# Conditioning blocks in runs of four, and the state store issued from SyncE

## The chip, the core and the metric

The kernel runs on one NeuronCore of a Trainium2 chip. The metric is the device time of one execution in microseconds (us); the time before is the median of three executions. A profiled execution gives the rows shown further down; times inside it count from the start of its span.

## The reference, cut to what matters

One inference step of a two-layer trunk over 128 context and 256 latent tokens, width 1024. Layer 0 mixes tokens with a bidirectional state-space scan (SSD: 32 heads of width 64, 8 groups, state 128, chunks of 128 tokens), layer 1 with a gated delta rule; each is followed by a convolutional feed-forward. All sub-layers are modulated by vectors that come from a condition:

```python
def adaln_params(cond, w_ada, b_ada):
    ada = (jax.nn.silu(cond) @ w_ada + b_ada)[:, None, :]
    return tuple(jnp.split(ada, 6, axis=-1))
...
# ssd_scan, one direction
decay = jnp.exp(jnp.where(mask, seg, -jnp.inf))
y_intra = jnp.einsum('bcijgr,bcjgrp->bcigrp', scores[..., None] * decay, xdt)
states = jnp.einsum('bcqgn,bcqgr,bcqgrp->bcgrpn', bc, decay_end, xdt)
y_inter = jnp.einsum('bcign,bcgrpn,bcigr->bcigrp', cc, s_prev, jnp.exp(acum))
```

The final states of the context scan are outputs of their own (`new_state_ssd_fwd`, `new_state_ssd_bwd`). The product with `w_ada` (2 layers x 6 x 1024 columns, 96 blocks of 1024x128 in float32, 512 KB each) uses only two condition vectors, so it is nearly all weight traffic.

## The kernel before, in words

The first 16 blocks of `w_ada` are used ahead of layer 0. The other 80 are used inside the SSD scan, `ADA_G`: ten in each of its eight groups g = 0 to 7. Every engine has its program written out by hand; they meet only at semaphores.

**Buffers and loads.** Weight blocks go through `raw`, `RAW` = 4 buffers used in turn. `load_block` (L252, its DMA is L259) runs on SyncE (SP) and waits until the block four places earlier has been used (`ada_used`), so block 4 of a group is asked for when its block 0 is used, and block 0 of the next group when block 6 is. `ssd_sp` (L884) issues, per group: the load of the next group's start states `s0` (L895, 256 KB), then ten block loads.

**TensorE (`ssd_pe`, L1054).** A group covers three token chunks, u = 3g, 3g+1, 3g+2. `turn_rows` (L1065, L1066) transposes a chunk into PSUM bank 0 and waits for `s_gm` of the chunk before; `segment` (L1075, L1076) makes the decay exponents; `states` (L1086) the group's context states; `entry_decays` (L1099) the decays at chunk entry, and with k = 0 it waits until ScalarE has copied the states out (`s_stout`), since it overwrites their bank; `entry` (L1111) the part of the output that comes from the entry state; `outputs` (L1124) the part inside the chunk. `conditioning(g, lo, hi)` (L1130) runs blocks lo to hi of the group's ten through `ada_block` (L369, 8 matmuls a block, each block after the wait for its load). `ada_columns` (L376) ends the group after ScalarE has copied the ten rows out (L396).

Between `segment(u+1)` and the group's end the order before is: states, blocks 0-1, entry_decays 0, outputs u, blocks 2-3, turn_rows u+3, segment u+2, entry_decays 1, blocks 4-5, entry 0, turn_rows u+4, blocks 6-7, outputs u+1, turn_rows u+5, segment u+3, entry 1, blocks 8-9, outputs u+2, ada_columns. In the last group the runs are 0-1, 2-4, 5-7, 8-9, with no `turn_rows`, no `segment(u+3)` and no run after entry 1.

**ScalarE (`ssd_act`, L900).** In order: `decays` (exp of a segment, L913), `state_out` (L919, states to `st_sb`), `rows_lo` (L946, eight activations, `seg_lo`), the store of `st_sb` to `o_ssd` (L962, its own DMA queue), `entry_decays` (L925), `token_rows` (L909, `xtok`), `decays`, `gates_out` (L931 or L935, L937), `entry_decays`, `rows_lo`, `token_rows` twice, `decays`, `rows_lo`, `ada_rows` (L396). `state_out` of the next group waits until the store has landed (`s_out`).

**VectorE (`ssd_dve`).** `masked` (L1177, `gm_s`) follows `xtok` of its chunk and frees PSUM bank 0 for the next `turn_rows`; `entered` (L1203, L1204, L1206) takes the result of `entry`. VectorE runs `entered(g, 0)` ahead of `masked(u+4)`.

After the last group SyncE has loaded the first blocks of `w_out`; ScalarE rounds them to the high part (`whi`, L277), GpSimd makes the low part (`wlo`, L287), and the output product (L327) starts.

Of the kernel before, what the change touches and what calls it, by code (L numbers as in the profile page):

```python
# [49 lines left out]
SSD_H, SSD_P, SSD_G = 32, 64, 8  # L50
# [68 lines left out]
def trunk(nc, io):  # L119
    ctx = ExitStack()  # L120
    with ctx:
        def sem(name):
            return ctx.enter_context(nc.semaphore(name))
# [62 lines left out]
        def v(name):  # L186
            a, b = VEC[name]
            return vec[:, a:b]
# [63 lines left out]
        def load_block(sp, p, j):  # L252
            b = j + p.raw0
            if j.i is not None or j.base >= RAW:
                sp.wait_ge(ada_used if p.kind == "ada" else lo_ready, (j + (p.own0 - RAW + 1)).val)
            elif b.base >= RAW:
                s, count = used(b.base - RAW)
                sp.wait_ge(s, count + 1)
            sp.dma_start(raw[:, b.mod(RAW), 0:p.kt * P], p.src[j.val]).then_inc(raw_in[b.mod(RAW)], 16)  # L259
# [5 lines left out]
        def load_first(sp, p):  # L265
            for k in range(RAW):
                load_block(sp, p, Idx(k))
# [11 lines left out]
        def split_first(act, name):  # L279

            for k in range(2):
                split_hi(act, phase[name], Idx(k))
# [112 lines left out]
        def ada_rows(act, bank, n):  # L395
            act.activation(arow[:, :], ps[:, bank, 0:P], ACT.Copy).then_inc(ada_row, 1)  # L396
# [438 lines left out]
        def tmp(name, shape, dt=F32):  # L835
            t = put(name, shape, dt, at=st[0])
            st[0] += nbytes([P] + list(shape[1:]), dt)
            assert st[0] <= rows_at, (name, st[0], rows_at)
            return t
# [13 lines left out]
        st_sb = tmp("st_sb", [P, 512])  # L853
        ADA_G = tuple(10 * g for g in range(SSD_G)) + (ADA_2,)
        s_s0 = [sem(f"s_s0{k}") for k in range(2)]
        s_out = [sem(f"s_out{k}") for k in range(2)]
# [20 lines left out]
        def ssd_begin(eng):  # L877
            eng.wait_ge(dt_last, 1)
            eng.wait_ge(tok_split, 2)
            eng.wait_ge(dt_dec, 1)  # L880
            eng.wait_ge(conv_silu, 2 + CONV_T)
            eng.wait_ge(blk_done, phase["ssd_in"].own0 + N_IN + SPL)

        def ssd_sp(sp):  # L884
            p = phase["ada_rest"]
            load_first(sp, p)
            ssd_begin(sp)
            sp.dma_start(s0[:, 0, :, :], io["s_ssd"][0]).then_inc(s_s0[0], 16)
            for g in range(SSD_G):
                b = g % 2  # L890
                if g + 1 < SSD_G:
                    if g:
                        sp.wait_ge(s_in, 2 * g)
                        sp.wait_ge(s_dec, 2 * g)
                    sp.dma_start(s0[:, 1 - b, :, :], io["s_ssd"][g + 1]).then_inc(s_s0[1 - b], 16)  # L895
                for j in range(ADA_G[g] + RAW, min(ADA_G[g + 1] + RAW, ADA_2)):
                    load_block(sp, p, Idx(j))
            load_first(sp, phase["ssd_out"])

        def ssd_act(act):  # L900
            ssd_begin(act)

            def token_rows(u):
                g, c = u // 3, u % 3
                act.wait_ge(s_a, u + 1)
                if g >= 2:
                    act.wait_ge(s_xdt, u - 5)
                    act.wait_ge(s_st, 2 * g - 2)
                act.activation(xtok[:, g % 2, c, :], ps[:, 0, 0:TOK], ACT.Copy).then_inc(s_xtok, 1)  # L909

            def decays(u):
                act.wait_ge(s_seg, u + 1)
                act.activation(ps[:, 1 + u % 2, :], ps[:, 1 + u % 2, :], ACT.Exp).then_inc(s_exp, 1)  # L913

            def state_out(g):
                act.wait_ge(s_st, 2 * g + 1)
                if g:
                    act.wait_ge(s_out[(g - 1) % 2], 16 * ((g - 1) // 2 + 1))
                act.activation(st_sb[:, :], ps[:, 4, :], ACT.Copy).then_inc(s_stout, 1)  # L919

            def entry_decays(g, k):
                act.wait_ge(s_eb, 2 * g + k + 1)
                if g:
                    act.wait_ge(s_bw, 2 * g - 1 + k)
                act.activation(e_in[:, k].rearrange("p d n -> p (d n)"), ps[:, 4 + k, :], ACT.Exp).then_inc(s_ee, 1)  # L925

            def gates_out(g):
                act.wait_ge(s_v, 3 * g + 3)
                for t in (2 * g, 2 * g + 1):
                    if g == 0:  # L930
                        act.activation(rms_sum[t % 2][:, :], gate[:, t, :], ACT.Square).then_inc(rms_sq, 1)  # L931
                    else:
                        if g > 1:
                            act.wait_ge(rms_add, t - 3)
                        act.activation(rms_new[t % 2][:, :], gate[:, t, :], ACT.Square).then_inc(rms_sq, 1)  # L935
                for t in (2 * g, 2 * g + 1):
                    act.activation(yhi[:, t, :], gate[:, t, :], ACT.Copy, scale=nw[:, t:t + 1]).then_inc(y_hi, 1)  # L937

            def rows_lo(u):
                g, c = u // 3, u % 3  # L940
                if u:
                    act.wait_ge(s_seg, u)
                for d in range(2):
                    for h in range(4):
                        n = 4 * g + 32 * d + h
                        i = act.activation(seg_lo[:, d, h * P:(h + 1) * P], masks[:, 1 + d, :], ACT.Copy,  # L946
                                           scale=tok_lo[:, c, n:n + 1].bitcast(F32))
                i.then_inc(s_rlo, 1)

            nw = v("ssd_norm")  # L950
            rows_lo(0)
            for c in range(NCH):
                token_rows(c)
            decays(0)
            rows_lo(1)
            for g in range(SSD_G):
                more = g + 1 < SSD_G
                decays(3 * g + 1)
                state_out(g)
                rows_lo(3 * g + 2)  # L960
                act.wait_ge(s_stout, g + 1)
                act.dma_start(io["o_ssd"][g], st_sb[:, :].rearrange("p (d n) -> p d n", d=2)).then_inc(s_out[g % 2], 16)  # L962
                entry_decays(g, 0)
                if more:
                    token_rows(3 * g + 3)
                decays(3 * g + 2)
                if g:
                    gates_out(g - 1)
                entry_decays(g, 1)
                if more:  # L970
                    rows_lo(3 * g + 3)
                    token_rows(3 * g + 4)
                    token_rows(3 * g + 5)
                    decays(3 * g + 3)
                    rows_lo(3 * g + 4)
                act.wait_ge(ada_used, ADA_1 + ADA_G[g + 1])
                act.wait_ge(ada_tr, g + 1)
                ada_rows(act, 3, ADA_G[g + 1] - ADA_G[g])
            split_first(act, "ssd_out")
            gates_out(SSD_G - 1)  # L980
# [73 lines left out]
        def ssd_pe(pe):  # L1054
            ssd_begin(pe)
            p = phase["ada_rest"]
# [73 lines left out]
            def conditioning(g, lo, hi):  # L1130
                if lo == 0:
                    pe.wait_ge(ada_ready, g + 2)
                count = ADA_G[g + 1] - ADA_G[g]
                for n in range(min(lo, count), min(hi, count)):
                    ada_block(pe, Idx(p.raw0 + ADA_G[g] + n), 3, n, count)
# [4 lines left out]
            for g in range(SSD_G):  # L1140
                u = 3 * g
                segment(u + 1)
                last = g + 1 == SSD_G
                states(g)
                conditioning(g, 0, 2)
                entry_decays(g, 0)
                outputs(u)
                conditioning(g, 2, 5 if last else 4)
                turn_rows(u + 3)
                segment(u + 2)  # L1150
                entry_decays(g, 1)
                conditioning(g, 5 if last else 4, 8 if last else 6)
                entry(g, 0)
                turn_rows(u + 4)
                conditioning(g, 8 if last else 6, 10 if last else 8)
                outputs(u + 1)
                turn_rows(u + 5)
                if g + 1 < SSD_G:
                    segment(u + 3)
                entry(g, 1)  # L1160
                if g + 1 < SSD_G:
                    conditioning(g, 8, 10)
                outputs(u + 2)
                pe.wait_ge(ada_row, g + 2)
                ada_columns(pe, ADA_G[g + 1] - ADA_G[g], 3)
# [1529 lines left out]
```

## Time and profile before

| | |
|---|---|
| median of three executions | 1739.4 us (1738.55 to 1741.45) |
| the profiled execution's own time | 1738.55 us |
| its span, first to last instruction | 1736.8 us |
| TensorE busy | 1590.8 us, 92% of the span |
| mean granted TensorE clock | 0.952 of full speed |
| SSD scan on TensorE | about 255 to 426 us |

A group is known by its number g. Its start is the first `states` matmul: 288.89, 308.65, 328.42, 348.17, 367.91 and 387.66 us for g = 1 to 6. "Landing" is the time from the issue of a DMA to its last byte's semaphore.

### The profile page before, as it was taken

What the parts mean: (1) busy time and instruction counts of PE and PEld (TensorE: products, weight loads), DVE (VectorE), ACT (ScalarE), POOL (GpSimd) and SP (SyncE); (2) the same over time, 40 slices, a digit from 0 to 9 for tenths busy, and PEclk for the clock granted to TensorE, in tenths of its full rate; (3) what the DMA queues carried; (4) which work ended last, traced back from release to release, by engine and by line L of the source; (5) the groups of instructions that cost most, each with busy time, mean ns of one, the idle gap of its engine ahead of it and who ended that gap; (6) DMA issues with size and microseconds to landing.
All of it is one profiled execution on the core that took longest, in us unless ns stands there. A gap on an engine that the chain in (4) does not pass through costs nothing.

```text
span 1736.8 us, 31461 instructions
## 1 busy us (share of the span) xinstructions
PE 1590.8 (92%) x11787; PEld 1484.4 (85%) x11787; DVE 909.6 (52%) x1753; ACT 765.7 (44%) x1370; POOL 911.0 (52%) x516
## 2 busy tenths in 40 slices
PE   4999999998978999998799999988988969999995
PEld 2999987777968999997699999878788949999994
DVE  1533105666237777523733455778873266777424
ACT  2555436765224444323546553544443334444322
POOL 1455555775533555553345555777563515555551
PEclk6999999999998999999899999899879979999998
DMA  8333336888322333432223232000013313343420
GB/s 326 105 111 127 128 122 221 290 297 274 110 85 79 127 123 131 143 124 73 97 98 110 98 100 66 18 14 25 14 50 109 121 48 109 121 132 131 134 100 36
DMA packets 54969, 205.26 MB, mean 118 GB/s; under 512 B 6096, under 2 KB 6096, under 8 KB 54352
## 3 DMA queue, kind: packets, MB, share of 16 engines
q1 hardware_dynamic: 53712, 201.70, 34.7%
q10 hardware_dynamic: 1152, 2.10, 0.3%
q8 instruction: 73, 1.20, 0.3%
q14 instruction: 32, 0.26, 0.0%
HBM read 196.44 MB, written 7.34 MB: 117 GB/s over the span
## 4 chain that ended last, share of the span: by engine, by line
PE 50%; issue 23%; POOL 12%; DVE 7%; ACT 6%; DMA 1%; POOLq 0%; DVEq 0%; SPq 0%; ACTq 0%
POOL wlo L287 12%; PE ps L327 5%; PE ps L329 5%; PE ps L328 5%; PE ps L780 4%; PE ps L782 4%; PE ps L781 4%; PE ps L2379 3%; PE ps L2381 3%; PE ps L2380 3%; ACT seg_lo L946 2%; PE ps L369 1%; PE ps L1471 1%; PE ps L1086 1%; PE ps L1573 1%
## 5 line engine op out<-in xcount | busy, mean ns | idle before, releaser
L287 POOL TENSOR_TENSOR wlo<-raw,whi 128x1024 fp32r<-128x1024 f32 (+1 forms) x201 | 511.2, 2544 | 496.7 <-ACT whi L277 496.7
L277 ACT ACTIVATE whi<-raw 128x1024 fp32r<-128x1024 f32 (+1 forms) x250 | 275.2, 1102 | 603.9 <-PE ps L329 376.7
L327 PE MATMUL ps<-hhi,whi 128*128 128x384 f32 x704 | 238.5, 339 | 25.5 <-DVE hlo L434 25.4
L328 PE MATMUL ps<-hlo,whi 128*128 128x384 f32 x704 | 236.5, 336 | 0.0
L329 PE MATMUL ps<-hhi,wlo 128*128 128x384 f32 x704 | 236.5, 336 | 0.0
L611 DVE SCALAR_TENSOR_TENSOR evac<-ps,vec,evac 128x189 f32<-128x189 f32 (+3 forms) x440 | 166.4, 412 | 101.7 <-ACT evac L562 72.0
L2168 POOL TENSOR_TENSOR wlo<-raw,whi 128x1024 fp32r<-128x1024 f32 x49 | 118.2, 2413 | 140.5 <-ACT whi L277 140.5
L544 DVE SCALAR_TENSOR_TENSOR xr<-xr,evac 128x384 f32 x32 | 64.1, 2004 | 195.1 <-ACT evac L513 193.9
L327 PEld LDWEIGHTS ps<-hhi,whi 128*128 128x128 f32 x704 | 133.0, 189 | 31.2 <-issue 29.8
L2379 PE MATMUL ps<-hhi,whi 128*128 128x384 f32 x392 | 140.4, 358 | 12.9 <-DVE hlo L434 12.3
L780 PE MATMUL ps<-hhi,whi 128*128 128x384 f32 x392 | 133.3, 340 | 10.2 <-DVE hlo L434 9.6
L328 PEld LDWEIGHTS ps<-hlo,whi 128*128 128x128 f32 x704 | 133.4, 189 | 0.0
L329 PEld LDWEIGHTS ps<-hhi,wlo 128*128 128x128 f32 x704 | 133.2, 189 | 0.0
L2381 PE MATMUL ps<-hhi,wlo 128*128 128x384 f32 x392 | 132.7, 339 | 0.0
L2380 PE MATMUL ps<-hlo,whi 128*128 128x384 f32 x392 | 132.7, 338 | 0.0
L782 PE MATMUL ps<-hhi,wlo 128*128 128x384 f32 x392 | 132.1, 337 | 0.0
L781 PE MATMUL ps<-hlo,whi 128*128 128x384 f32 x392 | 132.1, 337 | 0.0
L327 PE MATMUL ps<-ghi,whi 128*128 128x384 f32 x352 | 121.3, 345 | 1.3 <-POOL wlo L287 1.3
L329 PE MATMUL ps<-ghi,wlo 128*128 128x384 f32 x352 | 117.6, 334 | 0.0
L328 PE MATMUL ps<-glo,whi 128*128 128x384 f32 x352 | 117.6, 334 | 0.0
L327 PE MATMUL ps<-yhi,whi 128*128 128x384 f32 x256 | 90.3, 353 | 3.5 <-POOL wlo L287 3.5
L2379 PEld LDWEIGHTS ps<-hhi,whi 128*128 128x128 f32 x392 | 74.6, 190 | 19.1 <-issue 16.4
(306 smaller groups left out, 3426.2 us busy)
## 6 DMA issues: line engine op xcount, KB each, us to landing
raw<-w_in_in SPq DMA_DIRECT2D x98, 512.0 KB, 3.5
raw<-w_ada_in SPq DMA_DIRECT2D x96, 512.0 KB, 4.9
raw<-w_up_in SPq DMA_DIRECT2D x88, 512.0 KB, 3.4
raw<-w_down_in SPq DMA_DIRECT2D x32, 704.0 KB, 4.1
raw<-w_out_in SPq DMA_DIRECT2D x32, 512.0 KB, 3.4
s<-s_ssd_in SPq DMA_DIRECT2D x8, 256.0 KB, 4.9
o_ssd_out<-st_sb ACTq DMA_DIRECT2D x8, 256.0 KB, 2.3
S<-s_gdn_in SPq DMA_DIRECT2D x4, 512.0 KB, 3.4
```

Of the source, the lines that this page charges most:

```text
L277: act.activation(whi[:, s.mod(SPL), 0:p.kt * P], raw[:, b.mod(RAW), 0:p.kt * P], ACT.Copy).then_inc(hi_ready, 1)
L287: pool.tensor_tensor(wlo[:, s.mod(SPL), 0:p.kt * P], raw[:, b.mod(RAW), 0:p.kt * P], whi[:, s.mod(SPL), 0:p.kt * P].bitcast(F32), ALU.subt ...
L327: pe.matmul(out, a, rhi[:, h, :], start=(r == 0), stop=False)
L328: pe.matmul(out, a, rlo[:, lo_tile(r) if lo_tile else r, :], start=False, stop=False)
L329: mm = pe.matmul(out, b, rhi[:, h, :], start=False, stop=(r == q * p.kt - 1))
L611: i = dve.scalar_tensor_tensor(x, y, w, x, ALU.mult, ALU.add)
L780: pe.matmul(out, a, hhi[:, k, :], start=(k == 0), stop=False)
L781: pe.matmul(out, a, hlo[:, k, :], start=False, stop=False)
L782: mm = pe.matmul(out, b, hhi[:, k, :], start=False, stop=(k == DT - 1))
L2379: pe.matmul(out, a, hhi[:, k, :], start=(k == 0), stop=False)
L2380: pe.matmul(out, a, hlo[:, k, :], start=False, stop=False)
L2381: mm = pe.matmul(out, b, hhi[:, k, :], start=False, stop=(k == DT - 1))
```

## The change

SyncE takes the store over from ScalarE: for each group it waits for `s_stout` after the load of `s0` and issues the store ahead of the group's ten block loads. On TensorE the ten blocks run as 0-3 behind `states`, 4-7 behind entry_decays 1, and 8-9 behind entry 1; in the last group as 0-3 and 4-9. Matmuls, loads and bytes are the same in number and kind.

```diff
@@ ssd_sp
                     sp.dma_start(s0[:, 1 - b, :, :], io["s_ssd"][g + 1]).then_inc(s_s0[1 - b], 16)
+                sp.wait_ge(s_stout, g + 1)
+                sp.dma_start(io["o_ssd"][g], st_sb[:, :].rearrange("p (d n) -> p d n", d=2)).then_inc(s_out[b], 16)
                 for j in range(ADA_G[g] + RAW, min(ADA_G[g + 1] + RAW, ADA_2)):
@@ ssd_act
                 rows_lo(3 * g + 2)
-                act.wait_ge(s_stout, g + 1)
-                act.dma_start(io["o_ssd"][g], st_sb[:, :].rearrange("p (d n) -> p d n", d=2)).then_inc(s_out[g % 2], 16)
                 entry_decays(g, 0)
@@ ssd_pe
                 segment(u + 1)
-                last = g + 1 == SSD_G
                 states(g)
-                conditioning(g, 0, 2)
+                conditioning(g, 0, 4)
                 entry_decays(g, 0)
                 outputs(u)
-                conditioning(g, 2, 5 if last else 4)
                 turn_rows(u + 3)
                 segment(u + 2)
                 entry_decays(g, 1)
-                conditioning(g, 5 if last else 4, 8 if last else 6)
+                conditioning(g, 4, 8 if g + 1 < SSD_G else 10)
                 entry(g, 0)
                 turn_rows(u + 4)
-                conditioning(g, 8 if last else 6, 10 if last else 8)
                 outputs(u + 1)
```

## Rows read from the trace of the kernel before

**Rows 1.** The page: span, busy time, granted TensorE clock in 40 slices of 43.4 us.

```profile
span 1736.8 us, 31461 instructions
...
PEclk6999999999998999999899999899879979999998
```

**Rows 2.** Busy time by window: PE, PEld, DVE, ACT, POOL, then clock, DMA share, GB/s.

```profile
288.90:308.65 19.75, 19.02 (x295) 15.68 (x294) 13.52 (x29) 13.79 (x38) 12.48 (x13) 1.00 0.85 297
...
407.40:430.00 22.60, 17.31 (x277) 13.44 (x276) 13.22 (x29) 11.09 (x24) 9.63 (x7) 1.00 0.77 269
```

**Rows 3.** TensorE's timeline in group 1: start, length, line, operation, [idle before].

```profile
288.89 1.89 PE L1086 MATMUL ps<-xw,xtok 128*128 128x256 f32 x8
290.71 1.08 PE L369 MATMUL ps<-raw,scond 128*32 128x128 f32 x32
...
297.28 1.08 PE L369 MATMUL ps<-raw,scond 128*32 128x128 f32 x32
298.29 1.16 PE L1111 MATMUL ps<-proj,s 128*128 128x128 f32 x8
...
299.93 1.08 PE L369 MATMUL ps<-raw,scond 128*32 128x128 f32 x32
300.94 1.09 PE L1124 MATMUL ps<-ge_s,xdt 128*64 128x128 f32 x16
302.51 0.55 PE L1065 MATMUL ps<-masks,proj 128*128 128x128 f32 x3 [0.47 <-DVE gm_s L1177]
```

**Rows 4.** ScalarE's timeline in group 1, around the store, and its later L946.

```profile
289.95 0.60 ACT L919 ACTIVATE st_sb<-ps 128x512 f32<-128x512 f32 x1 [0.28 <-PE ps L1086]
...
290.58 0.34 ACTq L962 DMA_DIRECT2D o_ssd_out<-st_sb  x1
290.74 2.14 ACT L946 ACTIVATE seg_lo<-masks,tok_lo 128x128 fp32r<-128x128 f32 x7
...
295.43 0.49 ACT L909 ACTIVATE xtok<-ps 128x384 f32<-128x384 f32 x1 [1.98 <-PE ps L1066]
...
299.18 2.44 ACT L946 ACTIVATE seg_lo<-masks,tok_lo 128x128 fp32r<-128x128 f32 x8
```

**Rows 5.** VectorE's timeline in group 1: `masked(u+3)`, start of `entered(g, 0)`, `masked(u+4)`.

```profile
295.96 0.42 DVE L1177 TENSOR_TENSOR gm_s<-ps,masks 128x256 f32<-128x256 f32 x1 [1.16 <-ACT xtok L909]
...
300.10 0.42 DVE L1203 TENSOR_TENSOR ps<-ps,e_in 128x256 f32<-128x256 f32 x1
...
302.03 0.42 DVE L1177 TENSOR_TENSOR gm_s<-ps,masks 128x256 f32<-128x256 f32 x1 [0.72 <-ACT xtok L909]
```

**Rows 6.** Loads of blocks 4 and 5 of group 1, then of its blocks 6 and 7.

```profile
L259 SPq DMA_DIRECT2D raw<-w_ada_in x2: 327/362/396, 291.4 to 291.9; - x2
DMA to landing us min/median/max: 3.7/4.7/5.6
L259 SPq DMA_DIRECT2D raw<-w_ada_in x2: 327/619/911, 294.3 to 294.8; - x2
DMA to landing us min/median/max: 4.4/4.8/5.2
```

**Rows 7.** Loads of blocks 6 and 7 of group 6.

```profile
L259 SPq DMA_DIRECT2D raw<-w_ada_in x2: 328/348/368, 393.1 to 393.5; - x2
DMA to landing us min/median/max: 4.9/5.3/5.7
```

**Rows 8.** Loads of group 3's blocks 2 and 3, issued at the end of group 2.

```profile
L259 SPq DMA_DIRECT2D raw<-w_ada_in x2: 328/348/367, 325.5 to 325.9; - x2
DMA to landing us min/median/max: 4.2/5.0/5.8
```

**Rows 9.** DMA traffic in 40 slices of 288.89 to 308.65 us.

```profile
GB/s 423 415 402 390 158 340 203 133 274 315 307 423 390 373 323 415 373 365 323 141 191 182 282 307 373 357 274 224 323 265 390 431 423 207 108 66 116 232 257 406
```

**Rows 10.** The end of the last group: PE's timeline, then the chain that ended last.

```profile
428.96 0.44 PE L327 MATMUL ps<-yhi,whi 128*128 128x384 f32 x1 [2.60 <-POOL wlo L287]
...
419.17 6.23 DMA raw<-w_out_in
```

## The prediction

> **What bounds the kernel now.** I read the page first: the span is 1736.8 us in 40 slices of 43.4 us, and TensorE is granted nearly its full clock after the first slice [rows 1]. The diff touches only the SSD scan, so next came the busy time by window, one window for each group; that of group 1 stands for six. What to see there: a group takes 19.75 us, TensorE is busy for 19.0 of it at a granted clock of 1.00, which is the 2.4 GHz level, and the DMA engines are 85% busy at 297 GB/s; only the last group is longer [rows 2]. So the scan is TensorE's, with DMA close behind. Any gain must come out of the 0.7 us in a group in which TensorE is idle, and a loss can come from loads.
>
> TensorE's timeline shows where that idle time is: 0.47 us before `turn_rows(u+5)`, for `gm_s` [rows 3]. `gm_s` itself waits for ScalarE's `xtok`, which stands behind the eight L946 activations of 2.44 us [rows 4, 5]. That chain starts where `segment(u+2)` ends, and the change leaves the same TensorE work ahead of that point (four blocks, entry_decays 0, outputs u, turn_rows). I take from this that the period of 19.75 us stays as it is unless a load comes late.
>
> **The store.** The part that goes: one wait and one DMA issue on ScalarE per group. The issue is 0.34 us long, but it runs beside the activations: seven L946 beside it take 2.14 us, 0.306 each, and eight without a store beside them 2.44 us, 0.305 each [rows 4]. The gain on ScalarE is 0. The wait costs nothing either, since `st_sb` is ready at 290.55 when the issue comes at 290.58.
>
> What is added on SyncE: a wait for `s_stout`, behind which the group's ten block loads queue, and for them TensorE waits. It ends at 290.55; the first load behind it can't go before block 0 is used and went at 291.4 [rows 4, 6]. The issue ends near 290.6 + 0.34 = 290.95, still 0.45 us ahead, so the wait costs 0. Uncovered, it would delay the load of block 4, which landed at 291.4 + 3.7 = 295.1 and is needed at 297.28, 2.2 us later [rows 3, 6].
>
> The Trainium skill (DMA: Bandwidth & Descriptors, section "Issuing engines are not separate DMA queues") says that issuing from several engines saves only the sequencer's issue time, as all queues run on the same 16 DMA engines. By that rule alone, taking the store off ScalarE's queue would be worth up to 8 x 0.34 = 2.7 us; the rows above put it at 0, because the issue lies beside activations that are as long without it.
>
> **Blocks 0-3.** Blocks 2 and 3 now run right behind 0 and 1, ahead of entry_decays 0 and outputs u. A run of two takes 1.01 us (299.93 to 300.94), so 0.507 a block [rows 3]: counted from the group's start, block 2 is needed at 1.82 + 1.01 = 2.83 and block 3 at 3.34. Their loads are asked for when blocks 8 and 9 of the group before are used, which doesn't move. The worst pair was issued at 325.5 and 325.9 and landed at 329.7 and 331.7 [rows 8]; group 3 starts at 328.42, so it needs them at 331.25 and 331.76: 0.06 us to spare. This is the tightest of seven such pairs; in the other six block 3 landed 0.5 to 1.5 us ahead of its new need. Cost 0. Entry_decays 0 and outputs u come 1.01 us later. VectorE, which idles 1.16 us behind them, before `masked(u+3)`, and ScalarE, idle 1.98 us between its `e_in` and the next `xtok`, absorb that [rows 4, 5]; the tighter has 0.15 us left.
>
> **Blocks 4-7.** This is where I expect the cost. All four must now be in by the time TensorE has reached them: 4 at 297.28, that is 8.39 from the start, then 8.90, 9.40 and 9.91. Before, blocks 6 and 7 were wanted from 299.93, 11.04 from the start [rows 3]. Their loads can be asked for 1.9 us earlier (block 2 was used by about 294.1 and its buffer's next load was issued at 294.3, against 292.4 now, as block 2 is used by 288.89 + 3.34 [rows 3, 6]), but an earlier request helps only if the DMA engines are free.
>
> They were not. A 512 KB block at the peak rate of about 415 GB/s takes 1.27 us [rows 9]. In group 1 blocks 4 to 7 landed at 295.1, 297.5, 298.7 and 300.0, the last three 1.2 to 1.3 us apart, at the engines' pace [rows 6]. So block 7 has two bounds. Late: where it landed before, counted from the start 11.1, 11.05, 11.7, 11.6, 10.8 and 11.55 in groups 1 to 6, the first and last of them shown [rows 6, 7]. Early: block 5's landing plus two transfers, block 5 having landed at 8.6, 7.85, 9.2, 9.15, 7.9 and 8.65, which gives 11.1, 10.4, 11.7, 11.7, 10.4 and 11.2.
>
> TensorE starts a block about 0.1 us after it lands, and block 7 is needed at 9.91. The stalls (landing + 0.1 - 9.91) are then 1.3, 1.25, 1.9, 1.8, 1.0 and 1.75 by the late bound, 9.0 together, and 1.3, 0.6, 1.9, 1.9, 0.6 and 1.4 by the early one, 7.7 together.
>
> Part of each is hidden. `entry(g, 0)` now stands behind the four blocks. Before, it ended at 299.45, VectorE took it up at 300.10 and idled 0.72 us just before `masked(u+4)` at 302.03, so ended `entered` at 301.31 [rows 3, 5]. With two more blocks ahead, `entry` ends at 300.46, `entered` (1.21 us) at 301.7, and 0.3 us are left. TensorE's own slack is the 0.47 us [rows 3]. The smaller counts: each stall less 0.3 goes into the period, because behind `turn_rows(u+5)` everything hangs together again. That is 9.0 - 1.8 = 7.2 and 7.7 - 1.8 = 5.9 us for six groups. Group 0, which starts with four blocks in place, I put at 0.5 (an estimate). One thing works against this: blocks 8, 9 and the next two are asked for earlier, so the next group starts with a shorter queue. Were block 5 always in by 7.85, the best that the six show, the early bound would give 6 x (0.6 - 0.3) + 0.3 = 2.1 us. I take 6.0, near the early sum, and keep 2 and 8 as ends.
>
> **Blocks 8 and 9, last group.** Blocks 8 and 9 are needed where they were and are asked for when 4 and 5 have been used, as before; their loads have over 5 us; cost 0. The last group already waits for DMA: its window is 22.6 us with TensorE busy for 17.3 [rows 2], and the output product starts at 428.96 because the first `w_out` block landed at 425.4, issued at 419.17 when block 6 had been used [rows 10]. Block 6 is used when it lands in both orders, so the end stays. Its outputs end about 1 us later on TensorE, inside the 2.60 us of idle. Cost 0, with 1 us either way.
>
> **The sum.** 0 (store) + 0 (blocks 0-3) + 6.0 (blocks 4-7) + 0 (last group) on the profiled execution's own 1738.55 us gives 1744.6. That execution is 0.85 us under the median of the runs, so 1745.4 us by the median.
>
> **Rivals.**
> 1. *The queue drains first.* With the next two blocks asked for earlier, blocks 4 to 7 find a nearly empty queue and the stalls stay within what VectorE and TensorE can hide: + 0 to 3.5 us, in the middle 1741.2. For it: traffic falls to 66 to 116 GB/s for some slices before the group ends [rows 9]. Against it: block 7 landed after 10.8 in all six, and 9.9 + 0.3 is wanted.
> 2. *The store blocks the loads.* In SyncE's queue it stands in front of block 4. If block 4's data could start only once the store had landed (290.58 + up to 3.1 us, plus about 2.1 us from issue to first data, 3.4 of an unqueued load less 1.27), it would land at 8.2 and block 7 at 12.0: a stall of 2.2, 1.9 net, in seven groups: + 13, 1752. Against it: loads in one queue follow at 1.2 us [rows 6]. The skill's same page (section "Queues, rings and completion order") says that a semaphore write lands only after every earlier write of its DMA engine, across queues; by that the store's writes stand ahead of block 4 in either version and moving it changes nothing. No run shows this so far.
> 3. *Not slower.* The refills run ahead far enough that no new stall appears and the last group's queue is shorter: its block waits go and the first `w_out` block lands up to 2.6 us sooner, until the outputs before it bind (2.60 us, and no later group to hide it). - 2.6, 1736.8. It decides from the point where block 7 lands by 10.2 in all groups. For it: the waits at the end are all DMA [rows 10]; against it, DMA there never paused.
>
> **Chances.** Forecast 0.57, rival 1 0.26, rival 2 0.08, rival 3 0.09. A change under 0.2%, 3.5 us, is about what a measurement of this kernel can't tell from none. Of the forecast 0.05 lies under that. Slower: 0.52 + 0.08 and 0.03 of rival 1's upper end = 0.63. Faster: 0.04 of rival 3, where the 0.7 us of idle in other groups shrinks too. Within: 0.33. The range runs from the lower part of rival 1 past my upper end of 8 us (1747.4) some way towards rival 2: 1740 to 1750. Below it lie rival 3 and a little of rival 1, above it most of rival 2, together under 0.2.
>
> **What the new profile would show.** Right: a DMA wait on L369 inside blocks 5 to 7 of most groups, over 1 us in some, `turn_rows(u+5)` released by `gm_s` later than 13.6 from the start, a group of 20.3 to 21 us; no stall in blocks 0-3; L946 still 2.44 us. Wrong: no wait at block 7 and 19.75 us a group (rival 1 or 3), or block 4 itself waited for (rival 2). An entry_decays 0 that waits on `s_stout`, or late outputs u that delay VectorE's `masked(u+3)`, would break my zeros.

## The result, and the profile after

The changed kernel takes 1749.8 us in the median of five executions (1748.95 to 1755.87) against 1739.4. The medians differ by 10.4 us; the ratio of the means is 1.0066, 95% interval 1.0043 to 1.0090, so 11.5 us slower (7.5 to 15.7). The direction and the mechanism were forecast; the size was not: 6.0 us were forecast, less than the interval's lower end. By the ratio the time lies at 1750.9 (1746.9 to 1755.1), just outside the range of 1740 to 1750. The profiled execution took 1750.2 us with a span of 1748.4.

Busy time by window (columns as in [rows 2]), for groups 1 and 6:

```profile
291.95:312.94 20.99, 19.39 (x294) 15.63 (x293) 13.61 (x29) 13.94 (x38) 12.51 (x13) 1.00 0.77 276
...
396.28:418.41 22.13, 19.17 (x295) 15.68 (x294) 13.60 (x29) 13.93 (x38) 14.40 (x15) 1.00 0.75 262
```

TensorE is busy about as long in a group as before (19.4 and 19.2 us against 19.0), at the same granted clock, but a group takes 20.99 or 22.13 us instead of 19.75, and the DMA engines are *less* busy, 0.77 and 0.75 against 0.85. Both engines now idle in turns. The starts of `states` give all periods, before and after:

| group | 0 | 1 | 2 | 3 | 4 | 5 | 6 | last, to the first output product |
|---|---|---|---|---|---|---|---|---|
| before | 19.99 | 19.76 | 19.77 | 19.75 | 19.74 | 19.75 | 19.77 | 21.53 |
| after | 22.23 | 20.99 | 20.53 | 21.54 | 20.88 | 20.39 | 22.13 | 20.25 |
| difference | 2.24 | 1.23 | 0.76 | 1.79 | 1.14 | 0.64 | 2.36 | -1.28 |

The sum is 8.9 us. The rest of the span's growth of 11.6 to 11.7 us lies where the two programs are the same: 0.8 us ahead of the scan, 2.0 behind it. In the profiles of this document the scan starts between 268.8 and 271.3 us, and what follows it takes 1307.6 to 1312.2 us, with the same work each time, so I don't give that rest a cause.

TensorE's timeline in group 1, to be laid beside [rows 3]:

```profile
291.95 1.89 PE L1086 MATMUL ps<-xw,xtok 128*128 128x256 f32 x8
293.77 1.95 PE L369 MATMUL ps<-raw,scond 128*32 128x128 f32 x64
...
300.20 1.33 PE L369 MATMUL ps<-raw,scond 128*32 128x128 f32 x32
302.17 0.65 PE L369 MATMUL ps<-raw,scond 128*32 128x128 f32 x16 [0.64 <-DMA raw<-w_ada_in]
303.41 0.65 PE L369 MATMUL ps<-raw,scond 128*32 128x128 f32 x16 [0.59 <-DMA raw<-w_ada_in]
303.99 1.16 PE L1111 MATMUL ps<-proj,s 128*128 128x128 f32 x8
...
306.78 0.55 PE L1065 MATMUL ps<-masks,proj 128*128 128x128 f32 x3
```

Blocks 0-3 run without a gap. Then block 6 and block 7 are each waited for, and block 7 starts 11.46 us after the group's start, where the prediction needed it at 9.91: 1.55 us late by that count, of which 1.23 went into the period. The loads behind it (SyncE's issues of blocks 4 to 7 and their landings, as [rows 6]):

```profile
L259 SPq DMA_DIRECT2D raw<-w_ada_in x4: 328/406/1982, 294.5 to 295.8; - x4
DMA to landing us min/median/max: 5.1/6.4/7.6
```

All four are asked for by 295.8, block 7 some 2 us earlier in the group than before. It landed at 295.8 + 7.6 = 303.4, 11.4 from the start; before it was 11.1. The earlier request bought nothing. The same group's DMA engines in 40 slices of 0.52 us, busy tenths and GB/s (as [rows 9]):

```profile
DMA  9997298597999999973699998899993000006979
GB/s 414 406 363 289 74 382 117 94 336 250 351 375 398 406 414 429 422 320 125 203 351 359 390 367 328 304 382 383 437 375 125 23 16 23 16 0 109 265 242 359
```

What to see: the slices at 0 to 23 GB/s, 2 to 5 us before the group's end. Nothing new can be asked for then: each of the four buffers holds a block that isn't used yet, or is taken by a load that is nearly done (block 1 of group 2, asked for 12.2 us after group 1's start, landed at 18.6). What traffic is left, 16 to 23 GB/s, is no more than one of 16 engines' share of 415 GB/s (26), and the trace has a single packet of 4 KB at a time there. The next loads go when blocks 8 and 9 are used, about 3 us before the end of the group. Before, the pause was shorter (207, 108, 66, 116 GB/s, [rows 9]).

### The profile page after: what moved, and what is told of

Same layout as the page of the kernel before. It is cut to its first block, busy times and chain, and to the rows that moved or that the text cites. A ratio compares the mean times of both kernels' runs of the same rounds, so it can differ in the third digit from the quotient of the medians.

```text
span 1748.4 us, 31461 instructions
## 1 busy us (share of the span) xinstructions
PE 1595.5 (91%) x11787; PEld 1487.8 (85%) x11787; DVE 905.6 (52%) x1753; ACT 767.0 (44%) x1370; POOL 910.8 (52%) x516
## 4 chain that ended last, share of the span: by engine, by line
PE 49%; issue 23%; POOL 12%; DVE 7%; DMA 4%; ACT 4%; POOLq 0%; SPq 0%; DVEq 0%; ACTq 0%
POOL wlo L287 12%; PE ps L327 5%; PE ps L329 5%; PE ps L328 5%; DMA raw<-w_ada_in 4%; PE ps L780 4%; PE ps L781 3%; PE ps L782 3%; PE ps L2376 3%; PE ps L2378 3%; PE ps L2377 3%; PE ps L369 1%; ACT seg_lo L948 1%; PE ps L1468 1%; PE ps L1570 1%
## 5 line engine op out<-in xcount | busy, mean ns | idle before, releaser
L2376 PE MATMUL ps<-hhi,whi 128*128 128x384 f32 x392 | 140.7, 359 | 12.7 <-DVE hlo L434 11.9
```

Source lines behind the costliest of these rows:

```text
L2376: pe.matmul(out, a, hhi[:, k, :], start=(k == 0), stop=False)
```

## The experiments

The scan's length is that of each kernel's one profile, from the first `states` to the first output product; before 160.1 us, changed 168.9. The ratios are to the kernel before.

| kernel | ratio (95%) | us by the ratio | scan, us | against 160.1 |
|---|---|---|---|---|
| changed | 1.0066 (1.0043 to 1.0090) | +11.5 | 168.9 | +8.9 |
| e1_store | 0.9997 (0.9986 to 1.0008) | -0.5 | 158.7 | -1.3 |
| e2_runs | 1.0058 (1.0041 to 1.0075) | +10.1 | 168.0 | +8.0 |
| e3_first | 0.9994 (0.9982 to 1.0005) | -1.0 | 160.3 | +0.2 |
| e4_second | 1.0034 (1.0021 to 1.0047) | +5.9 | 167.8 | +7.7 |
| e5_half_after | 0.9987 (0.9973 to 1.0001) | -2.3 | 158.8 | -1.3 |
| e6_half_before | 0.9968 (0.9950 to 0.9985) | -5.6 | 155.9 | -4.2 |
| e7_later | 0.9994 (0.9980 to 1.0008) | -1.0 | 159.9 | -0.2 |
| e8_split_rows | 0.9987 (0.9970 to 1.0004) | -2.3 | 156.1 | -4.0 |
| e9_split_first | 0.9990 (0.9978 to 1.0001) | -1.7 | 156.0 | -4.0 |
| e10_split_late | 0.9997 (0.9984 to 1.0010) | -0.5 | 156.7 | -3.4 |

**The parts of the change, one at a time.** Theory: blocks are needed before their transfers end. Rivals: the store in SyncE's queue, or the order of the work itself.

e1_store, the store alone:

```diff
 # ssd_sp
+                sp.wait_ge(s_stout, g + 1)
+                sp.dma_start(io["o_ssd"][g], ...).then_inc(s_out[b], 16)
 # ssd_act
-                act.wait_ge(s_stout, g + 1)
-                act.dma_start(io["o_ssd"][g], ...).then_inc(s_out[g % 2], 16)
```

> The kernel before with only the store moved to SyncE's queue. Late loads (my theory: the loss comes from blocks that are needed before their transfers end): no change, 1736 to 1743 us, the groups 1 to 6 at 19.75 us, blocks 4 and 5 landing as before give or take 1 us. Rival, the store ahead of block 4 in one queue delays the loads: 3 us or more slower, block 4 landing over 1 us later in most groups and waited for.

Measured 0.9997, and 19.74 to 19.77 us in five of the seven groups ahead of the last; one took 20.23 with a wait of 0.64 us at a block. The store costs and gains nothing that can be measured; the rival's 3 us lie outside the interval, whose upper end is 1.4 us.

e2_runs, the changed kernel without the two store edits, so only its three runs:

> The changed kernel with the store back on ScalarE's queue, so only the runs of four. Late loads: as slow as the changed kernel, 10 to 12 us over the kernel before, with waits for DMA at blocks 6 and 7 of 0.5 to 2 us. Rival, the store delays the loads: at most half of that loss is left.

Measured 1.0058, groups 1 to 6 at 19.91 to 21.32 us. The loss is there without the store. In group 4 three blocks in a row are waited for (TensorE's timeline):

```profile
363.46 0.65 PE L369 MATMUL ps<-raw,scond 128*32 128x128 f32 x16 [0.18 <-DMA raw<-w_ada_in]
364.72 0.65 PE L369 MATMUL ps<-raw,scond 128*32 128x128 f32 x16 [0.61 <-DMA raw<-w_ada_in]
365.98 0.64 PE L369 MATMUL ps<-raw,scond 128*32 128x128 f32 x16 [0.61 <-DMA raw<-w_ada_in]
```

They start 1.26 us apart, which is a block's transfer at full rate (512 KB at 415 GB/s, 1.27 us), not its 0.5 us of matmuls. TensorE runs at the pace of the DMA engines here.

e3_first, only the first run:

```diff
-                conditioning(g, 0, 2)
+                conditioning(g, 0, 4)
-                conditioning(g, 2, 5 if last else 4)
-                conditioning(g, 5 if last else 4, 8 if last else 6)
+                conditioning(g, 4, 8 if last else 6)
```

> The kernel before with only blocks 0-3 run together, then 4-5, 6-7 and 8-9 where they were. Late loads: blocks 6 and 7 are needed 11.0 us after the start and asked for earlier, so no stall over the 0.3 to 0.5 us that is hidden: 1737 to 1742 us. Rival, the order itself costs (entry_decays 0 and outputs u come 1 us later, so VectorE or ScalarE is late): 0.3 to 0.7 us a group, 3 to 5 us slower, without waits for DMA.

Measured 0.9994, no loss. Five of the groups 1 to 6 took 19.60 to 19.63 us, 0.15 less than before; group 4, with waits for blocks 4 and 5, 20.20.

```profile
310.09:329.69 19.60, 18.88 (x294) 15.74 (x293) 13.52 (x29) 13.80 (x38) 12.46 (x14) 1.00 0.87 298
```

So entry_decays 0 and outputs u, 1 us later, delay nobody. A run that falls away gives TensorE back 0.14 us, 0.07 for each of its two ends (four blocks in one run take 1.88 us to the next operation, 293.77 to 295.65 in the changed kernel, two runs of two 2 x 1.01). Within a run a block takes 0.44 us, not the 0.507 of the prediction, which counted the ends in.

e4_second, only the second run:

```diff
-                conditioning(g, 5 if last else 4, 8 if last else 6)
+                conditioning(g, 5 if last else 4, 10 if last else 8)
...
-                conditioning(g, 8 if last else 6, 10 if last else 8)
```

> The kernel before with only blocks 4-7 run together (0-1, 2-3, 4-7, 8-9). Late loads: block 7 is asked for as before, lands 11 to 11.7 us after the start and is needed at 9.9, so 1.0 to 1.8 us of stall, 0.3 of it hidden: 6 to 8 us slower, most of the whole change's loss. Rival, the order of blocks 0-3 or the store is the cause: under 2 us slower.

Measured 1.0034, 5.9 us by the ratio and 7.7 in the scan. (In the last group the run is 5-9.) Here the loads of blocks 6 and 7 are asked for where they were before, 5.4 and 5.9 us after the start, and block 7 starts at 11.4 again (TensorE in group 1, which began at 292.75):

```profile
302.92 0.65 PE L369 MATMUL ps<-raw,scond 128*32 128x128 f32 x16 [0.61 <-DMA raw<-w_ada_in]
304.18 0.65 PE L369 MATMUL ps<-raw,scond 128*32 128x128 f32 x16 [0.62 <-DMA raw<-w_ada_in]
```

Over groups 1 to 6 block 7 starts at 11.33 us on the mean in this kernel, with late requests, at 11.37 in e2_runs and 11.56 in the changed kernel, with early ones. So asking for it 2 us earlier made no difference here. The run 4-7 is enough to make most of the loss in the scan, 7.7 of 8.9 us; by the ratios it is 5.9 of 11.5, with intervals that overlap (1.0021 to 1.0047 against 1.0043 to 1.0090).

**Is it the DMA?** Two kernels in which the 80 loads fetch half their bytes, so that half of each weight block is left out and only the times mean something. e5_half_after is the changed kernel, e6_half_before the kernel before (their lines stand 3 lower in the file):

```diff
-            sp.dma_start(raw[:, b.mod(RAW), 0:p.kt * P], p.src[j.val])...
+            if p.name == "ada_rest":
+                sp.dma_start(raw[:, b.mod(RAW), 0:P * p.kt // 2], p.src[j.val][:, 0:P * p.kt // 2])...
```

> The changed kernel, with each of the 80 conditioning loads in the scan cut to the first half of its bytes (256 KB; the other half of the buffer is stale, so the conditioning values are other ones, same instructions). Late loads: the stalls at blocks 5 to 7 are gone, the groups take 19.5 to 19.8 us, and the whole is 1 to 4 us faster than the kernel before. Rival, the order of the work or the store costs something itself: at least 3 us over the kernel before are left, with groups over 20.2 us.

> The kernel before with the same halved loads, as control: groups 1 to 6 stay at 19.75 us, since no load was waited for there; the last group loses its waits for DMA and about 2.5 us. If the halving sped up groups 1 to 6 as well, contention between DMA and the engines would be part of the story.

With half the bytes the changed order takes 19.63 to 19.66 us in groups 1 to 6, and the order before 19.73 to 19.76. Group 1 of each by windows, then TensorE in group 1 of e5_half_after:

```profile
289.45:309.11 19.66, 18.77 (x295) 15.81 (x294) 13.66 (x29) 13.85 (x38) 12.52 (x13) 1.00 0.52 163
...
291.47:311.23 19.76, 19.04 (x295) 15.69 (x294) 13.54 (x29) 13.78 (x38) 12.48 (x13) 1.00 0.50 163
```

```profile
297.70 1.96 PE L372 MATMUL ps<-raw,scond 128*32 128x128 f32 x64
299.59 1.16 PE L1114 MATMUL ps<-proj,s 128*128 128x128 f32 x8
...
302.94 0.55 PE L1068 MATMUL ps<-masks,proj 128*128 128x128 f32 x3 [0.62 <-DVE gm_s L1177]
```

The stalls are gone, with every instruction in the same place: the loss is transfer time, and without it the changed order is 0.1 us a group *faster*. It isn't 0.28, two runs' worth, because the second run's gain goes into TensorE's wait for `gm_s`, 0.62 us here against 0.47 before. The control's groups didn't move, though blocks 5 of groups 3 and 4 had been waited for 0.20 us each in the kernel before, inside the slack; so DMA traffic itself doesn't slow the engines by an amount seen here.

This pair also shows when an early request does pay. With half the traffic block 7, asked for at 3.9 us or a little later (5.7 in one group), landed 8.3 us after the group's start on the mean of groups 1 to 6 in e5_half_after; asked for at 5.9 in e6_half_before, at 9.5. With the full traffic the same 2 us bought nothing.

The last group surprised me. In the order before it fell from 21.53 to 17.20 us, more than the 2.5 I expected. In the changed order it is 20.69, still with waits at half the bytes (TensorE's timeline, where L372 is `ada_block`):

```profile
418.64 0.64 PE L372 MATMUL ps<-raw,scond 128*32 128x128 f32 x16 [1.58 <-DMA raw<-w_ada_in]
421.44 0.88 PE L372 MATMUL ps<-raw,scond 128*32 128x128 f32 x16 [2.16 <-DMA raw<-w_ada_in]
```

Blocks 8 and 9 stand in one run with 4 and 5, whose buffers they take, so they can't be asked for until the run has begun. Block 8 was asked for at 415.8 and landed at 418.6, with nothing ahead of it: 2.8 us for 256 KB that take 0.6 to transfer: a run longer than the number of buffers waits for latency, not only for bandwidth. (Block 9, asked for at 416.3, took 5.2 us, with the first `w_out` loads issued right behind it.)

**Where the run stands.** e7_later puts the run 4-7 (4-9 in the last group) where blocks 6-7 were:

```diff
-                conditioning(g, 4, 8 if g + 1 < SSD_G else 10)
                 entry(g, 0)
                 turn_rows(u + 4)
+                conditioning(g, 4, 8 if g + 1 < SSD_G else 10)
```

> The changed kernel with the run 4-7 (4-9 in the last group) moved behind entry 0 and turn_rows u+4, where blocks 6-7 were. Late loads: block 7 is then needed about 11.6 us after the start, so only landings over that stall (0 to 0.5 us, mostly hidden): between 2 us faster and 3 us slower than the kernel before. Rival, it is the run of four that costs, wherever it stands (the four loads asked for in one burst): still 6 us or more slower.

Measured 0.9994. Three of groups 1 to 6 took 19.65 us, the others 19.80 to 20.13 with a single wait of 0.27 to 0.45 us each. The same four loads, asked for in the same burst, cost nothing when they are needed 1.6 us later (an unwaited block 7 starts at 11.23 here, at 9.59 in the changed order with half the bytes). It is the time of need that makes the loss.

**The other wait.** e8_split_rows takes the kernel before and puts ScalarE's copy of chunk u+4 between the halves of `rows_lo`:

```diff
-                    rows_lo(3 * g + 3)
+                    rows_lo(3 * g + 3, (0,))
                     token_rows(3 * g + 4)
+                    rows_lo(3 * g + 3, (1,))
```

> The kernel before with one edit on ScalarE: the xtok copy of chunk u+4 goes between the two halves of the eight seg_lo activations. If the wait of 0.47 us before turn_rows u+5 comes from xtok behind those activations, it goes, 0.3 to 0.47 us in each of groups 1 to 6: 2 to 3 us faster. If something else is late just behind it (seg_lo for the next segment), nothing changes.

The wait for `gm_s` is gone from all groups. Where no load was late, a group took 19.21 us, 0.54 less; the others 19.4 to 19.7, three of them with a wait of 0.23 to 0.61 us for one of blocks 7 to 9. The whole, 0.9987, is not told apart from no change, though the scan in this profile is 4.0 us shorter; 1.9 of that lies in the last group, which was 1.7 shorter in e1_store too, without this edit.

```profile
368.99:388.20 19.21, 18.96 (x294) 15.68 (x293) 13.51 (x29) 13.78 (x38) 14.39 (x15) 1.00 0.87 302
```

e9_split_first is e8 with the first run of e3; e10_split_late is e8 with blocks 0-3 in one run and 4-7 behind turn_rows u+4.

> The kernel before with blocks 0-3 in one run, which shortened a group from 19.75 to 19.6 us, and with the xtok copy of u+4 between the halves of seg_lo, which brought it down to 19.2 us where no load was late. If both add up, 19.1 us a group and 3 to 5 us faster than the kernel before. If the DMA queue binds now (5.9 MB a group need about 17 us of DMA time and come with gaps), waits for DMA appear at blocks 5 to 9 and it is 1 to 3 us faster, no more than either alone.

> The same split of seg_lo with blocks 0-3, then 4-7 behind turn_rows u+4, then 8-9, the last group as before. Late loads: 19.1 us a group where the blocks are in, stalls of up to 0.5 us at block 7 otherwise: between 0 and 4 us faster than the kernel before.

Measured 0.9990 and 0.9997. The groups took 19.1 to 19.5 us in e9, 18.95 to 20.08 in e10. Neither is shown to beat the kernel before; both are well ahead of the changed one. The best of e9's groups, 19.08 us, has both gains (19.21 less 0.13), so they do add where the loads allow it; the whole is 1.7 us faster by the ratio, 3.8 at most, where 3 to 5 were expected if both add up. In e10 groups with waits of 0.66 and 0.57 us for blocks took 20.07 and 19.72.

## Why the prediction was right in kind and short in size

- *The period stays unless a load is late, and what is late is block 7 behind the run 4-7.* Right: e4_second and e5_half_after show it from both sides. The step that failed is the size of the term for blocks 4-7 and group 0, below.
- *The store costs 0 and gains 0.* Right (e1_store). ScalarE's eight L946 took 2.44 us with the store gone, and the wait on SyncE held nothing back: block 4 was asked for at 294.5 in the changed kernel, 0.2 us after block 0 had been used. This agrees with the Trainium skill (DMA: Bandwidth & Descriptors, "Issuing engines are not separate DMA queues"): another issuing engine saves issue time only, and here that time lay beside other work.
- *Each stall less 0.3 us goes into the period.* Right in the outcome: 1.55 gave 1.23 in group 1, and each of groups 0 to 6 ended 9.5 us after its block 7 had started. But two of its numbers were off and cancel. In e5_half_after, where nothing is waited for, block 7 starts at 9.59 and not 9.91, and the group takes 19.65; so the true stalls are 0.32 us longer, and 0.55 of each is hidden. (The 0.1 us from a landing to TensorE's start was 0.04 too.) The limit is the one that was named. VectorE in group 1 of the changed kernel, beside [rows 5]:

```profile
305.18 0.43 DVE L1200 TENSOR_TENSOR ps<-ps,e_in 128x256 f32<-128x256 f32 x1 [2.08 <-PE ps L1111]
...
305.97 0.42 DVE L1203 TENSOR_TENSOR y_in<-y_in,ps 128x256 f32<-128x256 f32 x1
306.31 0.42 DVE L1174 TENSOR_TENSOR gm_s<-ps,masks 128x256 f32<-128x256 f32 x1
```

  `masked(u+4)` follows `entered` without a gap, where it had waited 0.72 us for `xtok`.
- *The step that failed is the size of the blocks 4-7 term.* I worked out a late bound (block 7 lands when it landed before: 7.2 us for groups 1 to 6) and an early one (block 5 plus two transfers: 5.9), added 0.5 for group 0, and then took 6.0 for all seven, under both sums (7.7 and 6.4), and kept 2 as an end. Measured were 10.2 us for the seven groups. In groups 1 to 5, where nothing else was late, it was 5.6 us, against 5.7 by the late bound and 4.8 by the early one: block 7 landed 11.31 us after the start on the mean there, 11.28 before. The late bound was the right one. The rest of the gap is group 0 (1.7 us over its 0.5) and group 6 (0.9 over its late bound), both below. An early request into a queue with the full traffic in it was worth nothing.
- *Group 0, put at 0.5 us.* It measured 2.24. The 0.5 had no row under it, though the trace before had one: block 7 of group 0 landed 11.8 us after its start, which by the late bound gives 0.9 (the group's blocks start 0.8 later than in group 1). Block 7 was waited for there too:

```profile
282.44 0.64 PE L369 MATMUL ps<-raw,scond 128*32 128x128 f32 x16 [1.84 <-DMA raw<-w_ada_in]
```

  It starts 12.7 us after the group's start in the changed kernel and in e2_runs, 12.9 in e4_second. About 0.3 us is that the first matmuls of this group ran at a lower granted clock (0.95 over the group): block 0 starts 2.93 us after the start, against 2.59 before and 1.82 in all later groups, and all requests stand behind it. That start varies by itself, from 2.4 to 3.5 us over the kernels here; with 3.5, in e9_split_first, group 0 took 21.1 us without a wait for a load. The rest, a landing of block 7 up to 2.6 us behind block 6's in the changed kernel, I can't explain.
- *Blocks 0-3 cost 0, with 0.06 us to spare in the worst pair.* Right in six of the seven groups ahead of the last. In group 6 block 3 was waited for 1.40 us, and the group grew by 2.36. One profile doesn't say how often that happens; single waits of 0.27 to 0.66 us at block 3 in one group each of e2_runs, e7_later and e10_split_late say that it is not rare. A cover of 0.06 us should have been priced, and it was none: at 0.44 us a block, block 3 is wanted at 3.15 and not 3.34, so the pair of [rows 8], landed at 3.3, would have come about 0.2 us late.
- *The last group keeps its end.* It became 1.28 us shorter in the profile. In e1_store, which has the old order there, it was 1.7 us shorter too, so the scatter of landings is enough to explain it. Its zero held by that luck, not because the order is free there: with half the bytes the changed order took 20.69 and the order before 17.19.
- Rival 2 fell with e1_store, rivals 1 and 3 with e2_runs. Against rival 3 I had said that DMA never paused in the last group; the trace before has a pause there, 102 and 0 GB/s in two slices near 409 us. The queue did drain before a group's end, as rival 1 said, but that is idle time, not time gained.

## What to carry to other kernels

With a ring of N buffers, a load can be asked for only when its buffer comes free, so consuming in bursts makes both sides idle in turns: the DMA engines while the ring is full, the compute engine while it refills. Before joining uses of a stream into longer runs, work out for the last one in a run when it lands *by the DMA engines' pace* from the start of the burst, and compare that with its new time of need; asking earlier helped here only where the traffic ahead of it had pauses. Where the DMA engines are nearly as busy as the compute engine, as here, spread the uses evenly, don't let a run exceed the ring, and treat a cover of a few hundredths of a microsecond as none.

## What the runs showed of the hardware

- Joining two runs of 8-matmul blocks into one saved TensorE about 0.14 us (19.75 to 19.60-19.63 us a group in e3_first). With two runs joined (e5_half_after) the group kept 0.1 of 0.28; the rest became waiting for `gm_s`.
- Most DMA issues on SyncE took 0.33 to 0.44 us, but single ones much longer, and not at a fixed place in a burst: in the changed kernel 1.98 us for block 7 of group 1 and 1.03 to 1.14 for block 4 of groups 2, 3 and 5, in e2_runs 2.09 and 2.56 for block 6 of groups 1 and 4. The kernel before has them too (1.51 for block 7 of group 4). What such an issue waits for is open.
- A landing can wait for a single engine. In the changed kernel, 16.6 to 18.2 us after group 1's start, one packet of 4 KB at a time is under way (0.16 us each but the first, 26 GB/s while it lasts), and the load that was out landed at 18.6. Eight such packets take 1.27 us, the spacing of the landings. Near 302 us the traffic falls to 125 and 203 GB/s while two blocks that TensorE waits for are still out. That some engines had run dry there while others were behind is argued from that, not shown: the trace's packets don't name their engine.
- Halving the traffic (297 to 163 GB/s) left the period of the kernel before at 19.73 to 19.76 us: no contention between DMA and the compute engines can be seen here.
